# Expert stage of a two-block network: seven weight buffers, constants loaded one stage earlier, final sums of squares in column groups

## The chip, the cores and the metric

The kernel runs on one core of a Trainium2 chip, in float32. The metric is the device time of one execution in microseconds: 3112.23 us is the median of three runs before the change (3110.86 to 3115.06).

## What is computed

Two network blocks run one after the other on 512 tokens of width 1024. The change is in the last part of the second block: the merge of three branches with its residual, the router, a mixture of 16 experts and the last norm. In the reference this is

```python
merged = (sigmoid(gate_na) * (y_na @ w_branch_na) + sigmoid(gate_rw) * (y_rw @ w_branch_rw)
          + sigmoid(gate_mem) * (y_mem @ w_branch_mem))
x = x + merged @ w_out
h = rms_norm(x, norm_ffn_g)
affinity = softmax(h @ w_router)                    # 512 tokens x 16 experts
top_val, top_idx = top_k(affinity.T, 64)            # each expert takes its 64 best tokens
xe = h[top_idx]                                     # 16 x 64 x 1024
act = silu(xe @ w_gate) * (xe @ w_up)               # hidden width 2048
ye = (act @ w_down) * top_val                       # added back to the tokens taken
out = rms_norm(x + scattered(ye), norm_final_g)     # x / sqrt(mean(x*x) + 1e-6) * g
```

The weights of the 16 experts are 3 x 1024 x 2048 float32 values each, together 403 MB, all read once.

## The kernel before

The program is a row of stages, each a block with one instruction stream per engine. Between two blocks all engines meet at a barrier. Inside a block the order on an engine is the order in which the code is written, and engines wait for one another by counting semaphores. Names in the trace carry their stage: `merge_` is the function `merge_and_router`, `moe_` is `expert_ffn`; `acc` and `xg` live across both.

**The merge.** Eight branch tiles and then eight output tiles are computed on TensorE (PE), with weights (`merge_w`) loaded by SyncE (SP) into two buffers. After each output tile VectorE (DVE) adds the residual into `acc`, ScalarE (ACT) squares it (L3382) and scales it into `xg` (L3383), and TensorE multiplies `xg` with the router's weights in `route` (L3328): the eight tiles of 128 features go to four groups of 32 output partitions, which are summed later. At the end ACT copies these sums to `router_parts` (L3385) and DVE the tokens' sums of squares to `square_sums` (L3447).

**Routing.** `expert_ffn` first loads four small constants through SP (L3562: `select`, `ident`, `slots`, `gain`), then the expert weights. TensorE waits for all four (`loaded`), sums the router's four groups with `select` (L3580), and transposes tokens with `ident` (L3589). ACT makes the token scale with a logarithm and an exponential (L3728, L3730), each of which needs its own function table (ACT_TABLE_LOAD); it first waits for three memsets of DVE (`consts_ready`). DVE makes the softmax (L3800 to L3807), TensorE transposes it (L3597), and DVE copies it to `left` (L3819) and takes the 64 largest values of each expert in eight rounds of eight (L3821, L3822). The places become one-hot rows (`hot`, L3836), with which TensorE gathers the tokens (L3618) into `xe`, which lies in `xg`.

**Experts.** The hidden width is cut into 4 chunks of 512, so there are 64 chunks. A chunk `n` needs three pieces of weights, gate, up and down, of 128 x 4096 float32 = 2.097 MB each, 192 loads in all. SP issues them (L3570) into a ring of buffers:

```python
RING = 6
...
if i >= RING:                       # the piece that lay in this buffer must have been used
    if used_part == 2: sp.wait_ge(out_made, used + 1)
    else:              sp.wait_ge(hidden_made, used + 1)
```

The order of the pieces is gate 0, up 0, gate 1, up 1, down 0, gate 2, up 2, down 1, and so on. TensorE computes gate and up of a chunk side by side in two 64-partition halves of a bank (`hidden`, L3636), turns the product around (L3650), and multiplies with down (`output`, L3664). Every four chunks an expert is done; `combine` (L3689) spreads its 64 rows over the 512 tokens in four steps `q`, and DVE adds each step's two tiles into `acc` (L3861).

**The end.** After the last chunk the four steps of the last expert run. ACT squares the eight tiles of `acc` in the order in which they are done (L3778, into ring buffer 0). Then TensorE sums the squares over partitions, 8 matmuls with a 128 x 128 matrix of ones (L3716), ACT makes the scale (L3780 logarithm, L3782 exponential), DVE scales the eight tiles with `gain` (L3886), and SP stores each.

Of the kernel before, what the change touches and what calls it, by code (L numbers as in the profile page):

```python
# [7 lines left out]
P = 128  # L8
ALU = mybir.AluOpType
# [3214 lines left out]

def merge_and_router(nc, stage, y_drams, gate_dram, x_dram, w_dram, gain_dram, router_dram, acc, xg, router_parts, square_sums):

# [7 lines left out]
    with ExitStack() as ctx:  # L3234
# [15 lines left out]
        router = sb("router", [P, KT, P // ROUTER_GROUPS])  # L3250
        one = sb("one", [P, 1])
        bank = ps("bank", [P, 8, 512])

# [21 lines left out]
        sums_made = sem("sums_made")  # L3275
        parts_ready = sem("parts_ready")

        gv = gate_dram.rearrange("(b m p) t -> m p b t", b=3, p=P)
        xv = x_dram.rearrange("(m p) t -> p m t", p=P)

        with nc.Block() as block:

            @block.sync
            def _(sp):
                for g in range(tiles):
                    if g >= 2:
                        sp.wait_ge(w_ready, g - 1)
                    sp.dma_start(w[:, g % 2].rearrange("p k m -> p (k m)"), w_dram[g * P:(g + 1) * P, :]).then_inc(
                        w_loaded[g % 2], 16)
                    if g < KT:  # L3290
                        if g >= 2:
                            sp.wait_ge(gated_ready, g - 1)
                        sp.dma_start(gates[:, g % 2], gv[g]).then_inc(gates_loaded[g % 2], 16)
                    if g == 2:
                        sp.dma_start(gain[:], gain_dram).then_inc(small_loaded, 16)
                        sp.dma_start(router[:], router_dram).then_inc(small_loaded, 16)
                        sp.dma_start(acc[:], xv).then_inc(acc_loaded, 16)

            @block.tensor
# [47 lines left out]
            def _(act):  # L3347
# [27 lines left out]
                for g in range(KT, tiles):  # L3375
                    m = g - KT
                    if g + 1 < tiles:
                        split_w_high(g + 1)
                    act.wait_ge(acc_ready, m + 1)
                    if m >= 2:  # L3380
                        act.wait_ge(sq_added, m - 1)
                    nc.scalar.activation(sq[:, m % 2], acc[:, m], ACT.Square).then_inc(squared, 1)  # L3382
                    nc.scalar.activation(xg[:, m], acc[:, m], ACT.Copy, scale=gain[:, m:m + 1]).then_inc(xg_ready, 1)  # L3383
                act.wait_ge(routed, KT)
                nc.scalar.copy(router_parts[:], bank[:, 6]).then_inc(parts_ready, 1)  # L3385
# [68 lines left out]

def expert_ffn(nc, stage, acc, xg, router_parts, square_sums, select_dram, gate_dram, up_dram, down_dram, ident_dram, slots_dram,
               gain_dram, out_dram):

# [5 lines left out]
    FT = HALF // P  # L3463
    RING = 6
    BATCH = 4
    BATCHES = EXPERTS // BATCH
    CHUNKS_ALL = EXPERTS * FC
    WIDE = BATCH * CAPACITY
    with ExitStack() as ctx:
        sb, ps, sem = opener(nc, ctx, stage)  # L3470
# [6 lines left out]
        scatter = sb("scatter", [P, 2, T])  # L3477
        select = sb("select", [P, EXPERTS])
        token_scale = sb("token_scale", [P, TT])
        eps = sb("eps", [P, 1])  # L3480
        ident = sb("ident", [P, P])
        slots = sb("slots", [P, CAPACITY])
        logits = sb("logits", [P, TT, EXPERTS])
        high = sb("high", [P, TT])
        affinity = sb("affinity", [P, TT, EXPERTS])
        place_tok = sb("place_tok", [P, TT, EXPERTS])
        left = sb("left", [EXPERTS, T])
        best = sb("best", [EXPERTS, 8])
        chosen = sb("chosen", [EXPERTS, T])
        ones = sb("ones", [EXPERTS, T])  # L3490
        sg = sb("sg", [P, 2, HALF])
        act_t = sb("act_t", [P, 2, FT, CAPACITY])
        ye = sb("ye", [P, 2, HALF])
        gain = sb("gain", [P, KT])
        all_ones = sb("all_ones", [P, P])
        bank = ps("bank", [P, 8, 512])

        xe = xg[:].rearrange("p k t -> p (k t)").rearrange("p (b k n) -> p b k n", b=2, k=KT)
        sq = ring[:, 0].rearrange("p (k t) -> p k t", k=KT)
        scale = ring[:, 1, 0:T]  # L3500

        loaded = sem("loaded")
        consts_ready = sem("consts_ready")
# [26 lines left out]
        squared = sem("squared")  # L3530
        summed = sem("summed")
        final_log = sem("final_log")
        final_scale = sem("final_scale")
# [23 lines left out]
        with nc.Block() as block:  # L3557

            @block.sync
            def _(sp):  # L3560
                for dst, src in ((select[:], select_dram), (ident[:], ident_dram), (slots[:], slots_dram), (gain[:], gain_dram)):
                    sp.dma_start(dst, src).then_inc(loaded, 16)  # L3562
                for i, (n, part) in enumerate(items):
                    if i >= RING:
                        used, used_part = items[i - RING]
                        if used_part == 2:
                            sp.wait_ge(out_made, used + 1)
                        else:
                            sp.wait_ge(hidden_made, used + 1)
                    sp.dma_start(ring[:, i % RING], parts[part][n * P:(n + 1) * P, :]).then_inc(slot_loaded[i % RING], 16)  # L3570
                for j, m in enumerate(order_of):
                    sp.wait_ge(scaled, j + 1)
                    sp.dma_start(out_dram[m * P:(m + 1) * P, :], acc[:, m]).then_inc(stored, 16)
                sp.wait_ge(stored, 16 * KT)

            @block.tensor
            def _(pe):
                pe.wait_ge(loaded, 64)
                for t in range(TT):
# [116 lines left out]
                for n in range(CHUNKS_ALL + 1):  # L3696
# [13 lines left out]
                    if n >= FC + 1:  # L3710
                        combine((n - FC - 1) // FC, (n - FC - 1) % FC)
                for q in range(FT):
                    combine(EXPERTS - 1, q)
                for j, m in enumerate(order_of):
                    pe.wait_ge(squared, j + 1)
                    last = nc.tensor.matmul(bank[:, 3], all_ones[:], sq[:, m], start=(j == 0), stop=(j == KT - 1))  # L3716
                last.then_inc(summed, 1)

            @block.scalar
            def _(act):  # L3720
# [5 lines left out]

                act.wait_ge(consts_ready, 3)
                nc.scalar.activation(token_scale[:], square_sums[:], ACT.Ln, bias=eps[:, 0:1], scale=1.0 / D_MODEL).then_inc(scale_log, 1)  # L3728
# [47 lines left out]
                for j, m in enumerate(order_of):  # L3776
                    act.wait_ge(part_added, 2 * FT * (EXPERTS - 1) + j + 1)
                    nc.scalar.activation(sq[:, m], acc[:, m], ACT.Square).then_inc(squared, 1)  # L3778
                act.wait_ge(summed, 1)
                nc.scalar.activation(scale, bank[:, 3], ACT.Ln, bias=eps[:, 0:1], scale=1.0 / D_MODEL).then_inc(final_log, 1)  # L3780
                act.wait_ge(final_log, 1)
# [3 lines left out]
            def _(dve):  # L3785
                nc.vector.memset(eps[:], EPS).then_inc(consts_ready, 1)
                nc.vector.memset(all_ones[:], 1.0).then_inc(consts_ready, 1)
                nc.vector.memset(ones[:], 1.0).then_inc(consts_ready, 1)
                done = [0]
# [28 lines left out]
                dve.wait_ge(aff_turned, 1)  # L3818
                step(nc.vector.tensor_copy(left[:], bank[0:EXPERTS, 1]))  # L3819
                for r in range(CAPACITY // 8):  # L3820
                    step(nc.vector.max(best[:], left[:]))  # L3821
                    step(nc.vector.match_replace(left[:], best[:], left[:], -1.0))  # L3822
                    if r >= 1:
                        split_low(r)
                step(nc.vector.tensor_scalar(chosen[:], left[:], 0.0, None, ALU.is_lt))
                step(nc.vector.tensor_tensor_scan(left[:], ones[:], chosen[:], 0.0, ALU.mult, ALU.add))
                step(nc.vector.tensor_tensor(chosen[:], chosen[:], left[:], ALU.mult))
                assert done[0] == MOE_PLACES, done[0]
# [54 lines left out]
                dve.wait_ge(final_scale, 1)  # L3883
                dve.wait_ge(loaded, 64)
                for m in order_of:
# [21 lines left out]
def two_blocks(nc, d, out_dram):  # L3907
# [58 lines left out]
    with ExitStack() as keep:  # L3966
        acc = keep.enter_context(nc.sbuf_tensor("acc", [P, KT, SEQ], F32))
        xg = keep.enter_context(nc.sbuf_tensor("xg", [P, KT, SEQ], F32))
        router_parts = keep.enter_context(nc.sbuf_tensor("router_parts", [P, SEQ], F32))
        square_sums = keep.enter_context(nc.sbuf_tensor("square_sums", [P, SEQ // P], F32))  # L3970
        merge_and_router(nc, "merge_2", (y_na, y_mem, y_rw), g_all, x, d["w_merge_2"], d["norm_ffn_g_2"], d["router_2"], acc, xg,
                         router_parts, square_sums)
        expert_ffn(nc, "moe", acc, xg, router_parts, square_sums, d["select"], d["w_exp_gate_2"], d["w_exp_up_2"],
                   d["w_exp_down_2"], d["ident"], d["slots"], d["norm_final_g_2"], out_dram)

# [93 lines left out]
```

## Time and profile before

| | before |
|---|---|
| median of three runs | 3112.23 us (3110.86 to 3115.06) |
| the profiled execution's own time | 3112.08 us |
| its span in the profile | 3110.2 us |
| TensorE busy | 2737.7 us, 88% |
| VectorE busy | 1268.8 us, 41% |
| ScalarE busy | 801.1 us, 26% |
| DMA traffic | 628.49 MB, mean 202 GB/s |
| DMA traffic in the last third | 428 GB/s in nearly every slice |
| mean granted TensorE clock | 0.938 |

The span runs from the first to the last recorded instruction; the 1.9 us between it and the execution's time lie around it. Busy shares are means over stages with different limits: the expert stage is the last third of the span, and only there does the DMA run near 430 GB/s. Times inside the profile are microseconds from the span's start.

### The profile page before, as it was taken

What the parts mean: (1) busy time and instruction counts of PE and PEld (TensorE: products, weight loads), DVE (VectorE), ACT (ScalarE), POOL (GpSimd) and SP (SyncE); (2) the same over time, 40 slices, a digit from 0 to 9 for tenths busy, and PEclk for the clock granted to TensorE, in tenths of its full rate; (3) what the DMA queues carried; (4) which work ended last, traced back from release to release, by engine and by line L of the source; (5) the groups of instructions that cost most, each with busy time, mean ns of one, the idle gap of its engine ahead of it and who ended that gap; (6) DMA issues with size and microseconds to landing.
All of it is one profiled execution on the core that took longest, in us unless ns stands there. A gap on an engine that the chain in (4) does not pass through costs nothing. (4 is left out here: it accounts for less than half of the span.)

```text
span 3110.2 us, 45255 instructions
## 1 busy us (share of the span) xinstructions
PE 2737.7 (88%) x18876; PEld 1972.7 (63%) x18876; DVE 1268.8 (41%) x2146; ACT 801.1 (26%) x1295; POOL 110.6 (4%) x90
## 2 busy tenths in 40 slices
PE   7999877779799969899978999697899889998887
PEld 7999855479799969777867888474333333333332
DVE  5664565534256552366544333663111111111112
ACT  3212135433143331254333333342000000000001
POOL 0000011100000000000001222000000000000000
PEclk9999987789999989999989999898999999999999
DMA  4336530053433344333440000336999999999996
GB/s 136 134 134 155 119 128 21 21 198 124 147 101 115 105 151 123 105 128 130 150 152 29 1 2 1 141 116 257 428 427 428 428 427 428 428 427 428 428 428 254
DMA packets 212406, 628.49 MB, mean 202 GB/s; under 512 B 38464, under 2 KB 125632, under 8 KB 187200
## 3 DMA queue, kind: packets, MB, share of 16 engines
q1 hardware_dynamic: 179712, 573.06, 48.5%
q10 hardware_dynamic: 32512, 52.81, 4.8%
q8 instruction: 137, 2.24, 0.3%
q14 instruction: 45, 0.37, 0.0%
HBM read 577.74 MB, written 45.73 MB: 200 GB/s over the span
## 5 line engine op out<-in xcount | busy, mean ns | idle before, releaser
L3636 PE MATMUL moe_bank<-moe_ring,xg 128*64 128x512 f32 x2048 | 502.8, 636 | 93.8 <-DMA moe_ring<-in_w_exp_up 93.0
L3636 PEld LDWEIGHTS moe_bank<-moe_ring,xg 128*64 128x64 f32 x2048 | 157.4, 144 | 381.2 <-issue 372.7
L3853 DVE TENSOR_TENSOR moe_sg<-moe_sg,moe_bank 64x512 f32<-64x512 f32 x64 | 44.2, 690 | 596.6 <-ACT moe_sg L3747 596.6
L64 PE MATMUL in_bank<-in_x_low,in_w_high 128*128 128x264 f32 x896 | 259.5, 290 | 6.2 <-DVE in_w_low L1194 6.1
L66 PE MATMUL in_bank<-in_x_high,in_w_high 128*128 128x264 f32 x896 | 255.8, 286 | 0.0
L65 PE MATMUL in_bank<-in_x_high,in_w_low 128*128 128x264 f32 x896 | 255.8, 285 | 0.0
L3664 PE MATMUL moe_bank<-moe_ring,moe_act_t 128*64 128x512 f32 x1024 | 230.6, 592 | 0.5 <-ACT moe_act_t L3754 0.5
L64 PE MATMUL up_prod<-up_x_low,up_w_high 128*128 128x264 f32 x704 | 202.0, 287 | 0.0
L66 PE MATMUL up_prod<-up_x_high,up_w_high 128*128 128x264 f32 x704 | 200.9, 285 | 0.0
L65 PE MATMUL up_prod<-up_x_high,up_w_low 128*128 128x264 f32 x704 | 199.5, 283 | 0.0
L64 PEld LDWEIGHTS in_bank<-in_x_low,in_w_high 128*128 128x128 f32 x896 | 169.7, 189 | 8.2 <-DVE in_w_low L1194 7.4
L65 PEld LDWEIGHTS in_bank<-in_x_high,in_w_low 128*128 128x128 f32 x896 | 169.9, 190 | 0.3
L66 PEld LDWEIGHTS in_bank<-in_x_high,in_w_high 128*128 128x128 f32 x896 | 170.0, 190 | 0.0
L64 PE MATMUL merge_y<-merge_x_low,merge_w_high 128*128 128x264 f32 x512 | 147.6, 288 | 21.4 <-DVE merge_w_low L533 15.5
L3664 PEld LDWEIGHTS moe_bank<-moe_ring,moe_act_t 128*64 128x64 f32 x1024 | 73.4, 137 | 146.3 <-issue 145.7
L64 PE MATMUL front_bank<-front_x_low,front_w_high 128*128 128x512 f32 x368 | 148.6, 404 | 14.2 <-DVE front_w_low L2602 13.2
L3754 ACT COPY moe_act_t<-moe_bank 128x256 f32<-128x256 f32 x64 | 23.9, 373 | 527.4 <-PE moe_bank L3650 527.4
L3861 DVE TENSOR_TENSOR acc<-acc,moe_bank 128x512 f32<-128x512 f32 x128 | 82.1, 684 | 173.4 <-PE moe_bank L3689 173.4
L66 PE MATMUL merge_y<-merge_x_high,merge_w_high 128*128 128x264 f32 x512 | 146.9, 287 | 0.0
L65 PE MATMUL merge_y<-merge_x_high,merge_w_low 128*128 128x264 f32 x512 | 146.8, 287 | 0.0
L65 PE MATMUL front_bank<-front_x_high,front_w_low 128*128 128x512 f32 x368 | 144.5, 393 | 0.0
L66 PE MATMUL front_bank<-front_x_high,front_w_high 128*128 128x512 f32 x368 | 144.3, 392 | 0.0
(522 smaller groups left out, 5375.5 us busy)
## 6 DMA issues: line engine op xcount, KB each, us to landing
moe_ring<-in_w_exp_gate SPq DMA_DIRECT2D x64, 2048.0 KB, 16.7
moe_ring<-in_w_exp_up SPq DMA_DIRECT2D x64, 2048.0 KB, 21.2
moe_ring<-in_w_exp_down SPq DMA_DIRECT2D x64, 2048.0 KB, 23.0
in_w<-in_w_in SPq DMA_DIRECT2D x56, 512.0 KB, 3.5
front_w<-in_w_in SPq DMA_DIRECT2D x50, 512.0 KB, 3.4
up_w<-in_w_up SPq DMA_DIRECT2D x44, 512.0 KB, 5.1
p<-in_out ACTq DMA_DIRECT2D x48, 264.0 KB, 2.0
down_w<-in_w_down SPq DMA_DIRECT2D x8, 1408.0 KB, 8.9
```

Source lines behind the costliest of these rows:

```text
L64: nc.tensor.matmul(to, w_high, x_low, start=start, stop=False)
L65: nc.tensor.matmul(to, w_low, x_high, start=False, stop=False)
L66: return nc.tensor.matmul(to, w_high, x_high, start=False, stop=stop)
L3636: last = nc.tensor.matmul(bank[64 * g:64 * g + 64, s], xe[:, (e // BATCH) % 2, k, at:at + CAPACITY], ring[:, slot_of(n, g), k * HALF:(k + ...
L3664: last = nc.tensor.matmul(bank[64 * h:64 * h + 64, 3 + e % 2], act_t[:, s, j], ring[:, slot, at:at + HALF], start=(c == 0 and j == 0), sto ...
L3754: nc.scalar.copy(act_t[:, s].rearrange("p j n -> p (j n)"), bank[:, 2, s * FT * CAPACITY:(s + 1) * FT * CAPACITY]).then_inc(act_t_ready, 1)
L3853: nc.vector.tensor_tensor(sg[0:CAPACITY, s], sg[0:CAPACITY, s], bank[64:64 + CAPACITY, s], ALU.mult).then_inc(act_ready, 1)
L3861: nc.vector.tensor_tensor(acc[:, FT * h + q], acc[:, FT * h + q], bank[:, part_bank(e, q) + h], ALU.add).then_inc(part_added, 1)
```

## The change

Four edits, all in the merge and the expert stage:

1. `RING` is 7 instead of 6. To make room, `left`, `chosen` and `ones` are laid into `sg` and `ye`, which are not in use yet during routing.
2. The four constants are loaded during the merge, by SP after the weights of its ninth tile; the expert stage no longer waits for them.
3. ACT runs a logarithm of a single column at the end of the merge (`warm`), so that its function table is in place when the expert stage starts. DVE makes one more constant (`group_rows`, 1/32 everywhere) ahead of `ones`, and ACT waits for four memsets instead of three.
4. The final sums of squares are 8 matmuls of 32 output partitions (L3718 in the new file), the j-th into column group j mod 4, the first two ahead of the last combine. The four groups are copied to SBUF by ACT and summed and spread over all partitions by one more matmul with `group_rows` (L3729).

```diff
@@ merge_and_router, SP @@
                         sp.dma_start(acc[:], xv).then_inc(acc_loaded, 16)
+                    if g == KT:
+                        for dst, src in constants:
+                            sp.dma_start(dst, src).then_inc(constants_loaded, 16)
+                sp.wait_ge(constants_loaded, 16 * len(constants))
@@ merge_and_router, ACT @@
+                act.wait_ge(one_ready, 1)
+                nc.scalar.activation(warm[:], one[:], ACT.Ln).then_inc(parts_ready, 1)
                 act.wait_ge(routed, KT)
                 nc.scalar.copy(router_parts[:], bank[:, 6]).then_inc(parts_ready, 1)
@@ expert_ffn @@
-    RING = 6
+    RING = 7
+    GROUP = P // 4
...
+        sums = ring[:, 2, 0:T]
+        left, chosen, ones = sg[0:EXPERTS, 0], sg[0:EXPERTS, 1], ye[0:EXPERTS, 0]
@@ SP @@
-                for dst, src in ((select[:], select_dram), (ident[:], ident_dram), (slots[:], slots_dram), (gain[:], gain_dram)):
-                    sp.dma_start(dst, src).then_inc(loaded, 16)
@@ TensorE @@
-                pe.wait_ge(loaded, 64)
...
+                def sum_squares(j):
+                    pe.wait_ge(squared, j + 1)
+                    at = GROUP * (j % 4)
+                    nc.tensor.matmul(bank[at:at + GROUP, 3], all_ones[:, 0:GROUP], sq[:, order_of[j]], start=(j < 4),
+                                     stop=(j >= 4)).then_inc(summed, 1)
+
                 for q in range(FT):
                     combine(EXPERTS - 1, q)
-                for j, m in enumerate(order_of):
-                    pe.wait_ge(squared, j + 1)
-                    last = nc.tensor.matmul(bank[:, 3], all_ones[:], sq[:, m], start=(j == 0), stop=(j == KT - 1))
-                last.then_inc(summed, 1)
+                    if q >= 2:
+                        for j in range(2 * q - 4, 2 * q - 2):
+                            sum_squares(j)
+                for j in range(KT - 4, KT):
+                    sum_squares(j)
+                pe.wait_ge(sums_ready, 1)
+                nc.tensor.matmul(bank[:, 4], group_rows[:], sums, start=True, stop=True).then_inc(spread, 1)
@@ ACT @@
-                act.wait_ge(consts_ready, 3)
+                act.wait_ge(consts_ready, 4)
...
-                act.wait_ge(summed, 1)
-                nc.scalar.activation(scale, bank[:, 3], ACT.Ln, bias=eps[:, 0:1], scale=1.0 / D_MODEL).then_inc(final_log, 1)
+                act.wait_ge(summed, KT)
+                nc.scalar.copy(sums, bank[:, 3]).then_inc(sums_ready, 1)
+                act.wait_ge(spread, 1)
+                nc.scalar.activation(scale, bank[:, 4], ACT.Ln, bias=eps[:, 0:1], scale=1.0 / D_MODEL).then_inc(final_log, 1)
@@ DVE @@
+                nc.vector.memset(group_rows[:], 1.0 / GROUP).then_inc(consts_ready, 1)
-                nc.vector.memset(ones[:], 1.0).then_inc(consts_ready, 1)
+                nc.vector.memset(ones, 1.0).then_inc(consts_ready, 1)
```

On SyncE's queue, from the last merge weights to the first expert weights, before the change:

```order
L3293 DMA merge_gates<-p 128x3x512
L3288 DMA merge_w<-in_w_merge 128x1024 x8
L3281 UNCONDITIONAL_BRANCH
L3559 UNCONDITIONAL_BRANCH
L3562 DMA moe_select<-in_select 128x16
L3562 DMA moe_ident<-in_ident 128x128
L3562 DMA moe_slots<-in_slots 128x64
L3562 DMA moe_gain<-in_norm_final_g 128x8
L3570 DMA moe_ring<-in_w_exp_gate 128x4096
```

and with it:

```order
L3296 DMA merge_gates<-p 128x3x512
L3291 DMA merge_w<-in_w_merge 128x1024
L3303 DMA select<-in_select 128x16
L3303 DMA ident<-in_ident 128x128
L3303 DMA slots<-in_slots 128x64
L3303 DMA final_gain<-in_norm_final_g 128x8
L3291 DMA merge_w<-in_w_merge 128x1024 x7
L3284 UNCONDITIONAL_BRANCH
L3565 UNCONDITIONAL_BRANCH
L3574 DMA moe_ring<-in_w_exp_gate 128x4096
L3574 DMA moe_ring<-in_w_exp_up 128x4096
```

The four constants now stand between the ninth and the tenth load of merge weights, and the expert weights are the first DMAs after the barrier (the two branches are the ends of the blocks).

On ScalarE, from the end of the merge to the token scale, before:

```order
L3383 ACTIVATE xg<-acc,merge_gain 128x512
L3385 COPY router_parts<-merge_bank 128x512
L3281 UNCONDITIONAL_BRANCH
L3719 UNCONDITIONAL_BRANCH
L3728 ACT_TABLE_LOAD
L3728 ACTIVATE moe_token_scale<-square_sums,moe_eps 128x4
L3730 ACT_TABLE_LOAD
```

and with the change:

```order
L3390 ACTIVATE xg<-acc,merge_gain 128x512
L3392 ACT_TABLE_LOAD
L3392 ACTIVATE merge_warm<-merge_one 128x1
L3394 COPY router_parts<-merge_bank 128x512
L3284 UNCONDITIONAL_BRANCH
L3731 UNCONDITIONAL_BRANCH
L3740 ACTIVATE moe_token_scale<-square_sums,moe_eps 128x4
L3742 ACT_TABLE_LOAD
L3742 ACTIVATE moe_token_scale<-moe_token_scale 128x4
```

One of the two table loads, the one for the logarithm, has moved ahead of the copy of `router_parts`, together with a small logarithm of `merge_one`.

On TensorE, the last instructions of the program, before:

```order
L3689 MATMUL moe_bank<-moe_scatter,moe_ye 128x512 x2
L3650 MATMUL moe_bank<-moe_ident,moe_sg 128x64 x4
L3664 MATMUL moe_bank<-moe_ring,moe_act_t 64x512 x8
L3689 MATMUL moe_bank<-moe_scatter,moe_ye 128x512 x10
L3716 MATMUL moe_bank<-moe_ring,moe_all_ones 128x512 x8
```

and with the change:

```order
L3653 MATMUL moe_bank<-ident,moe_sg 128x64 x4
L3667 MATMUL moe_bank<-moe_ring,moe_act_t 64x512 x8
L3692 MATMUL moe_bank<-moe_scatter,moe_ye 128x512 x8
L3718 MATMUL moe_bank<-moe_ring,moe_all_ones 32x512 x2
L3692 MATMUL moe_bank<-moe_scatter,moe_ye 128x512 x2
L3718 MATMUL moe_bank<-moe_ring,moe_all_ones 32x512 x6
L3729 MATMUL moe_bank<-moe_ring,moe_group_rows 128x512
```

Two of the eight sums (now 32 output partitions instead of 128) stand ahead of the last expert's last combine, six behind it, and one matmul over all partitions follows.

## Rows read from the trace of the kernel before

**Rows 1.** Weight stream by stretch: us; busy PE, PEld, DVE, ACT, POOL; clock, DMA share, GB/s.

```profile
2113.00:2142.00 29.00, 11.50 (x53) 9.68 (x53) 23.15 (x45) 5.61 (x9) 0.00 (x0) 0.56 1.00 425
2142.50:2158.50 16.00, 15.28 (x90) 10.99 (x91) 0.00 (x0) 3.63 (x5) 0.00 (x0) 0.89 0.00 0
2163.00:3063.00 900.00, 807.23 (x3670) 287.76 (x3668) 137.00 (x207) 74.73 (x150) 0.00 (x0) 0.96 1.01 428
```

**Rows 2.** SyncE's queue in order of time: start us, us, instruction.

```profile
2109.20 0.33 SPq L3562 DMA_DIRECT2D moe_select<-in_select  x1
...
2113.88 0.46 SPq L3570 DMA_DIRECT2D moe_ring<-in_w_exp_gate  x1
2158.70 0.33 SPq L3570 DMA_DIRECT2D moe_ring<-in_w_exp_up  x1
```

**Rows 3.** Chain of waits, first and last expert chunks: start us, us, what.

```profile
2151.58 10.52 PE moe_bank L3636 x48
...
3046.98 21.19 DMA moe_ring<-in_w_exp_up
...
3068.30 3.65 PE moe_bank L3636 x16
```

**Rows 4.** All engines in order of time, from merge to routing.

```profile
2105.94 0.71 ACT L3383 ACTIVATE xg<-acc,merge_gain 128x512 f32<-128x512 f32 x1
2107.79 0.59 ACT L3385 COPY router_parts<-merge_bank 128x512 f32<-128x512 f32 x1 [1.14 <-PE merge_bank L3328]
2108.77 0.16 DVE L3447 COPY square_sums<-merge_bank 128x4 f32<-128x4 f32 x1 [2.01 <-PE merge_bank L3343]
...
2109.55 0.48 DVE L3788 MEMSET moe_ones<- 16x512 f32 x1
2110.51 0.30 ACT L3728 ACTIVATE moe_token_scale<-square_sums,moe_eps 128x4 f32<-128x4 f32 x1
2110.83 1.28 ACT L3730 ACT_TABLE_LOAD   x1
2112.12 0.21 ACT L3730 ACTIVATE moe_token_scale<-moe_token_scale 128x4 f32<-128x4 f32 x1
...
2112.24 1.89 PE L3580 MATMUL moe_bank<-moe_select,router_parts 128*128 128x16 f32 x8 [3.51 <-DMA moe_gain<-in_norm_final_g]
2114.17 0.23 DVE L3800 TENSOR_TENSOR moe_logits<-moe_bank,moe_token_scale 128x64 f32<-128x64 f32 x1 [4.13 <-PE moe_bank L3580]
...
2115.16 0.69 ACT L3724 ACTIVATE moe_z_tok<-moe_bank,moe_token_scale 128x512 fp32r<-128x512 f32 x1 [2.84 <-PE moe_bank L3589]
2115.75 0.25 ACT L3734 ACTIVATE moe_logits<-moe_logits 128x64 f32<-128x64 f32 x1
...
2116.57 0.23 DVE L3807 TENSOR_TENSOR moe_affinity<-moe_logits,moe_high 128x64 f32<-128x64 f32 x1
...
2117.42 1.06 PE L3597 MATMUL moe_bank<-moe_ident,moe_affinity 128*16 128x128 f32 x4
...
2118.51 0.68 DVE L3819 COPY moe_left<-moe_bank 16x512 f32<-16x512 f32 x1 [0.93 <-PE moe_bank L3597]
```

**Rows 5.** TensorE in the merge, around one router matmul.

```profile
2091.28 1.05 PE L3328 MATMUL merge_bank<-xg,merge_router 128*32 128x512 f32 x2
2092.26 0.50 PE L64 MATMUL merge_bank<-merge_m_low,merge_w_high 128*128 128x512 f32 x1
```

**Rows 6.** VectorE, ScalarE and TensorE, the final sums.

```profile
3088.48 5.00 DVE L3861 TENSOR_TENSOR acc<-acc,moe_bank 128x512 f32<-128x512 f32 x8 [1.31 <-PE moe_bank L3689]
3089.26 4.88 ACT L3778 ACTIVATE moe_ring<-acc 128x512 f32<-128x512 f32 x8 [8.19 <-DVE acc L3861]
3099.25 0.69 ACT L3780 ACTIVATE moe_ring<-moe_bank,moe_eps 128x512 f32<-128x512 f32 x1 [3.80 <-PE moe_bank L3716]
3089.82 2.33 PE L3689 MATMUL moe_bank<-moe_scatter,moe_ye 64*128 64x512 f32 x8 [0.52 <-DVE acc L3861]
3092.07 7.13 PE L3716 MATMUL moe_bank<-moe_ring,moe_all_ones 128*128 128x512 f32 x16
```

More of the change, by code:

```diff
@@ L3222, with merge_and_router @@
 ROUTER_GROUPS = 4
-def merge_and_router(nc, stage, y_drams, gate_dram, x_dram, w_dram, gain_dram, router_dram, acc, xg, router_parts, square_sums):
+def merge_and_router(nc, stage, y_drams, gate_dram, x_dram, w_dram, gain_dram, router_dram, constants, acc, xg, router_parts,
+                     square_sums):
     T = SEQ
@@ L3251, in merge_and_router @@
         one = sb("one", [P, 1])
+        warm = sb("warm", [P, 1])
         bank = ps("bank", [P, 8, 512])
@@ L3276, in merge_and_router @@
         parts_ready = sem("parts_ready")
+        constants_loaded = sem("constants_loaded")
         gv = gate_dram.rearrange("(b m p) t -> m p b t", b=3, p=P)
@@ L3452, with expert_ffn @@
 EXPERT_FF = 2 * D_MODEL
-def expert_ffn(nc, stage, acc, xg, router_parts, square_sums, select_dram, gate_dram, up_dram, down_dram, ident_dram, slots_dram,
-               gain_dram, out_dram):
+def expert_ffn(nc, stage, acc, xg, router_parts, square_sums, select, ident, slots, gain, gate_dram, up_dram, down_dram, out_dram):
     T = SEQ
@@ L3477, in expert_ffn @@
         scatter = sb("scatter", [P, 2, T])
-        select = sb("select", [P, EXPERTS])
         token_scale = sb("token_scale", [P, TT])
         eps = sb("eps", [P, 1])
-        ident = sb("ident", [P, P])
-        slots = sb("slots", [P, CAPACITY])
         logits = sb("logits", [P, TT, EXPERTS])
@@ L3486, in expert_ffn @@
         place_tok = sb("place_tok", [P, TT, EXPERTS])
-        left = sb("left", [EXPERTS, T])
         best = sb("best", [EXPERTS, 8])
-        chosen = sb("chosen", [EXPERTS, T])
-        ones = sb("ones", [EXPERTS, T])
         sg = sb("sg", [P, 2, HALF])
@@ L3493, in expert_ffn @@
         ye = sb("ye", [P, 2, HALF])
-        gain = sb("gain", [P, KT])
         all_ones = sb("all_ones", [P, P])
+        group_rows = sb("group_rows", [P, P])
         bank = ps("bank", [P, 8, 512])
@@ L3500, in expert_ffn @@
         scale = ring[:, 1, 0:T]
-        loaded = sem("loaded")
+        sums = ring[:, 2, 0:T]
+        left, chosen, ones = sg[0:EXPERTS, 0], sg[0:EXPERTS, 1], ye[0:EXPERTS, 0]
         consts_ready = sem("consts_ready")
@@ L3531, in expert_ffn @@
         summed = sem("summed")
+        sums_ready = sem("sums_ready")
+        spread = sem("spread")
         final_log = sem("final_log")
@@ L3818, in _ @@
                 dve.wait_ge(aff_turned, 1)
-                step(nc.vector.tensor_copy(left[:], bank[0:EXPERTS, 1]))
+                step(nc.vector.tensor_copy(left, bank[0:EXPERTS, 1]))
                 for r in range(CAPACITY // 8):
-                    step(nc.vector.max(best[:], left[:]))
-                    step(nc.vector.match_replace(left[:], best[:], left[:], -1.0))
+                    step(nc.vector.max(best[:], left))
+                    step(nc.vector.match_replace(left, best[:], left, -1.0))
                     if r >= 1:
                         split_low(r)
-                step(nc.vector.tensor_scalar(chosen[:], left[:], 0.0, None, ALU.is_lt))
-                step(nc.vector.tensor_tensor_scan(left[:], ones[:], chosen[:], 0.0, ALU.mult, ALU.add))
-                step(nc.vector.tensor_tensor(chosen[:], chosen[:], left[:], ALU.mult))
+                step(nc.vector.tensor_scalar(chosen, left, 0.0, None, ALU.is_lt))
+                step(nc.vector.tensor_tensor_scan(left, ones, chosen, 0.0, ALU.mult, ALU.add))
+                step(nc.vector.tensor_tensor(chosen, chosen, left, ALU.mult))
                 assert done[0] == MOE_PLACES, done[0]
@@ L3883, in _ @@
                 dve.wait_ge(final_scale, 1)
-                dve.wait_ge(loaded, 64)
                 for m in order_of:
@@ L3970, in two_blocks @@
         square_sums = keep.enter_context(nc.sbuf_tensor("square_sums", [P, SEQ // P], F32))
[L3971 to L3974, printed above, removed]
+        select = keep.enter_context(nc.sbuf_tensor("select", [P, EXPERTS], F32))
+        ident = keep.enter_context(nc.sbuf_tensor("ident", [P, P], F32))
+        slots = keep.enter_context(nc.sbuf_tensor("slots", [P, CAPACITY], F32))
+        gain = keep.enter_context(nc.sbuf_tensor("final_gain", [P, KT], F32))
+        constants = ((select[:], d["select"]), (ident[:], d["ident"]), (slots[:], d["slots"]), (gain[:], d["norm_final_g_2"]))
+        merge_and_router(nc, "merge_2", (y_na, y_mem, y_rw), g_all, x, d["w_merge_2"], d["norm_ffn_g_2"], d["router_2"], constants,
+                         acc, xg, router_parts, square_sums)
+        expert_ffn(nc, "moe", acc, xg, router_parts, square_sums, select, ident, slots, gain, d["w_exp_gate_2"], d["w_exp_up_2"],
+                   d["w_exp_down_2"], out_dram)
 def by_partition(a):
```

## The prediction

> **What bounds the kernel now.** I read the busy shares by stretch first, then SyncE's queue at the two ends of the expert stage, then the chain of waits, and last all engines in order of time where the change touches them. The stretches show a stage with one limit: for 900 us the DMA engines are busy the whole time (share 1.01) at 428 GB/s, while TensorE has 807 us of work [rows 1]. A load of weights is 2.097 MB, so it takes 2.097 / 0.428 = 4.90 us, and 192 of them 941 us. The reader is to see where this stream does not run: from 2142.5 to 2158.5 it moves nothing [rows 1]. SyncE's queue says why: the sixth load is issued at 2113.88, and the seventh only at 2158.70, because it waits until the first chunk's matmuls have used their buffer [rows 2]. Those start at 2151.58 [rows 3], at the end of routing. So the stage is: routing, then the first `hidden`, then the stream restarts and runs without a break until the last chunk, whose matmuls start at 3068.30, when the load issued at 3046.98 has landed after 21.19 us [rows 3]. What follows is the tail. Three things can therefore move the end: how many loads are done before the restart, when the restart comes, and how long the tail is.
>
> **Edit 1, the seventh buffer.** The seventh load no longer waits. It is issued right behind the sixth and runs in the empty stretch, where there are 16 us for its 4.90 us [rows 1]. The restart then has 185 loads before it instead of 186. The stream has a backlog at every moment until the end (share 1.01), so the whole 4.90 us come off the landing of the last weights. Releases stay in time: the first chunk frees two buffers at once, 9.8 us of stream, and the next chunk's matmuls take less than that. In the steady stage a deeper ring buys nothing, since the DMA is full anyhow. **Minus 4.9 us.** Bounds: 0, if the last landing were not set by the restart, to 4.9; a loss is rival E.
>
> **Edits 2 and 3, an earlier start of routing.** Before, TensorE's first matmul starts at 2112.24 after 3.51 us in which it waited for the last constant [rows 4], while SyncE's first instruction after the barrier stands at 2109.20 [rows 2]. Without that wait it starts at about 2109.3, 2.9 us earlier. Its chain to the copy of `left` at 2118.51 [rows 4] is: router sums 1.89, then 3.3 of transposes, then the turn of `affinity` 1.06, together 6.24 us from 2112.24, which would end at 2115.5. The other chain into that turn goes through the token scale. Of the logarithm's two table loads one goes, but ACT now waits for four memsets, of which `ones` is the last: it started at 2109.55 and took 0.48 [rows 4]. A 128-column memset ahead of it adds about 0.2, so `ones` ends at 2110.25, and the logarithm starts there instead of at 2110.51. So the warm table saves 0.25 us, not 1.28. Logarithm 0.30, table load 1.28 and exponential 0.21 follow, and the scale stands at 2112.1 instead of 2112.33. The first softmax step then starts at 2112.2 instead of 2114.17. Before, the softmax's exponential waited for ACT's first token copy (2115.16 plus 0.69, exponential at 2115.75); now that copy starts with the scale at 2112.15, since the transposes are done by then, and the exponential runs at 2113.0. From exponential to the end of `affinity` it was 2115.75 to 2116.80, 1.05 us [rows 4], so `affinity` is there at 2114.0 and TensorE's transposes, ending at 2114.5, are the later of the two. The turn and the copy follow: `left` at about 2115.3, **3.2 us earlier**. From there to the first chunk's matmuls it is 2151.58 - 2118.51 = 33.1 us [rows 3, 4], mostly one long row of DVE steps in which nothing changes, and the restart comes as much earlier. Bounds: 2.5, if the barrier opens 0.4 later and the transposes run as slowly as before, to 3.9, if the granted clock, 0.56 in that stretch [rows 1], stays at its higher level because TensorE no longer idles. A part that starts at another clock phase in the gather is within that.
>
> What this moves elsewhere: the four constants stand on SyncE's queue in the merge, between the loads of the ninth and the tenth tile. Four issues like that of 2109.20, about 0.4 us each, delay the tenth load by under 2 us; the expert stage's own loads come 1.8 us earlier, which the empty stretch hides. I cost both at nothing; if the tenth tile had no slack, it would be 2 us. On ACT the warm-up stands in front of the copy of `router_parts`. The last scaling ends at 2105.94 + 0.71 = 2106.65; table load 1.28 and a small logarithm of 0.2 to 0.3 end at 2108.2; the copy, 0.59, ends at 2108.8 instead of 2108.38. DVE's last instruction ends at 2108.93 [rows 4], so the barrier stays where it was. **Nothing**, with 0.15 us to spare.
>
> The rows have no idle time around a table load: the logarithm ends at 2110.81, the load starts at 2110.83 and the exponential follows at 2112.12 [rows 4]. The Trainium skill (ScalarE: Activation LUTs, section "What ACT_TABLE_LOAD costs") adds a drain of about 1.38 us to each load of 1.28 us. By that rule the merge's barrier would come some 1.3 us later, and the sum would be 3104.1 as an estimate; the trace does not agree, and I give it little.
>
> **Edit 4, the sums.** Before: eight sums of 7.13 us start at 3092.07 behind the last combine, and the logarithm starts at 3099.25 [rows 6]. DVE's eight adds run without a gap from 3088.48, 0.625 each, and ACT's squares follow them, 0.61 each, to 3094.14 [rows 6]. After: the third combine ends at 3090.9 and the first two squares are ready at 3090.5. The two sums go into different column groups; the pairs of `hidden` and `combine` matmuls run side by side in this kernel: 8 records of combine, two combines, in 2.33 us [rows 6], where each record alone takes about 0.45 (7.13 / 16). So I take 1.0 us for two or four sums, until 3091.95. The last combine moves from 3091.01 to 3092.0 and ends at 3093.1, the last add at 3094.4, the last square at 3095.05, all 0.9 later than before. The middle four sums end by 3094.3, the last one at 3096.05. Then come the copy, 0.6 as that of `router_parts`, to 3096.7, and the spreading matmul, 0.9 plus 0.2 of hand-over, to 3097.85. The logarithm's table load, which before lay beside the sums, now follows the copy: 3096.7 + 1.28 = 3098.0. The logarithm starts there instead of at 3099.25: **minus 1.2 us**. Bounds: minus 2.1, if the first two sums don't hold the last combine up (last sum at 3095.15, then the same 1.95 us); plus 1.8, if the sums run one after another at 0.89 each (rival B).
>
> A change of tile shape costs little in the rows: a router matmul of 32 columns starts at 2091.28, and the next 128-column one 0.98 later [rows 5], against 0.89 for a float32 matmul in a row of its like [rows 6]. The Trainium skill (TensorEngine Tiling (Array Packing), section "Key Properties") says that a change of the tiling mode drains the engine, which speaks against sums put between combines. By the row that is 0.1 us for each of three changes; were it a whole matmul each time, the gain of 1.2 would be gone.
>
> **The sum.** 4.9 + 3.2 + 1.2 = 9.3 us, against the profiled execution's 3112.08, which is 0.15 below the median of the runs shown: 3102.8 us.
>
> **Rivals.**
> B. The column groups run one after another. Sums of 0.89 each: the last combine would end at 3093.9, the middle four at 3097.4, the last two at 3099.2, and with copy and spreading the logarithm would start at 3101.05, 1.8 late. Time 3105.8. For it: no row has four groups of 32 at once. Against: the combine rows.
> C. The last landing does not follow the restart, so the seventh buffer gives nothing: 3107.7. For it: a load takes 21.19 us to land, more than four at full rate, so its slowest part may run on another schedule. Against: no stall in 900 us.
> D. The barrier comes 1.3 us later through the warm-up: 3104.1.
> E. **Slower.** With one more load in flight the stream runs at a lower rate, through 185 loads or 906 us. It eats the gain of 9.3 from 1.03% on, 428 down to 423.6 GB/s; at 2% the time is 3102.8 + 18.1 = 3120.9. For it: nothing measured with seven. Against: 425 GB/s in the first fill, when the number in flight falls from six to none, and 428 later [rows 1].
> F. The change does not do what it says for routing, because the token scale decides and not the constants: 0.2 instead of 3.2, 3105.8.
>
> **How the numbers follow.** Forecast 0.76 (its own range 3100 to 3105.5), B 0.09, C 0.05, D 0.03, E 0.04, F 0.03. A measurement of this kernel tells about 0.2% from no change, 6.2 us, so faster is below 3106.0. That holds for the forecast, D and half of B and F: 0.85. C, the other halves and a small E are no change: 0.12. A large E is slower: 0.03. Runs of one kernel lie up to 3 us above their median, so the range goes from 3099.5 (upper bounds of all terms 3101.2, less 1.5 of run-to-run difference) to 3107.5, short of C.
>
> **What would show it.** Right: seven weight loads issued in a row right after the barrier, an empty stretch of about 10 us instead of 16 (16 - 4.9 + 1.8 - 3.2), the eighth load at about 2155.5, `left` at 2115.3, the last chunk's matmuls at about 3060.2, the logarithm 29.8 us behind them instead of 30.95. Wrong: a rate under 428 GB/s in the stage, sums of 0.9 us each, a barrier after 2109.2, or a last chunk less than 7 us earlier.

## The result and the profile after

The changed kernel takes 3095.57 us (median of six runs, 3093.32 to 3097.03) against 3113.64 us before (six runs, 3107.98 to 3118.66): a ratio of 0.9942, 95% interval 0.9930 to 0.9955. The forecast was 3102.8 with a range from 3099.5 to 3107.5: right in its sign, but the gain is 18 us and not 9.

Five marks in the two profiles cut the span into stretches:

| stretch | before | after | difference | forecast |
|---|---|---|---|---|
| start of the span to SyncE's first expert instruction | 2109.20 | 2108.71 | -0.5 | 0 |
| from there to the copy of `left` | 9.31 | 6.03 | -3.3 | -3.2 |
| to the first chunk's matmuls | 33.07 | 31.97 | -1.1 | 0 |
| to the first release of a buffer | 7.12 | 7.12 | 0 | 0 |
| to the landing of the last chunk's up weights | 909.47 | 898.38 | -11.1 | -4.9 |
| to the end of the span | 42.03 | 40.79 | -1.2 | -1.2 |
| span | 3110.2 | 3093.0 | -17.2 | -9.3 |

The weight stream by stretch, columns as in [rows 1]:

```profile
2144.00:2154.00 10.00, 9.28 (x51) 4.78 (x51) 0.00 (x0) 2.62 (x4) 0.00 (x0) 1.00 0.05 23
2163.00:3040.00 877.00, 786.57 (x3619) 281.65 (x3617) 136.28 (x206) 73.55 (x147) 0.00 (x0) 0.97 1.01 431
```

The long stretch runs at 431 GB/s where it ran at 428 [rows 1]. The window before the restart still holds the last packets of the first fill (23 GB/s); the stream itself stands still for some 9 us, where about 10 were forecast. The first fill does not differ: the 425 in [rows 1] is the mean of a window that takes in both ends of the fill. Inside it the rates are 433 before and 431 after:

```profile
2118.00:2136.00 18.00, 4.43 (x19) 2.94 (x16) 16.89 (x33) 3.10 (x5) 0.00 (x0) 0.59 1.01 433
2118.00:2136.00 18.00, 3.95 (x16) 2.64 (x16) 16.68 (x31) 2.06 (x3) 0.00 (x0) 0.54 1.01 431
```

SyncE's queue and the chain of waits, to be held against [rows 2, 3]:

```profile
2108.71 0.33 SPq L3574 DMA_DIRECT2D moe_ring<-in_w_exp_gate  x1
...
2111.98 0.47 SPq L3574 DMA_DIRECT2D moe_ring<-in_w_exp_up  x1
2153.83 0.33 SPq L3574 DMA_DIRECT2D moe_ring<-in_w_exp_down  x1
```

```profile
2146.71 10.52 PE moe_bank L3639 x48
...
3032.57 19.64 DMA moe_ring<-in_w_exp_up
...
3052.35 3.65 PE moe_bank L3639 x16
```

Seven loads go out in a row, the eighth 41.9 us later. 185 loads take 898.38 us, 4.856 each; before it was 186 loads in 909.47, 4.890 each. One load less is 4.9 us of the difference, the 0.033 us on each of 185 loads the other 6.2.

All engines between merge and routing, against [rows 4]:

```profile
2106.18 1.28 ACT L3392 ACT_TABLE_LOAD   x1
...
2107.58 0.57 ACT L3394 COPY router_parts<-merge_bank 128x512 f32<-128x512 f32 x1
2108.28 0.16 DVE L3456 COPY square_sums<-merge_bank 128x4 f32<-128x4 f32 x1 [2.01 <-PE merge_bank L3350]
...
2108.76 1.59 PE L3583 MATMUL moe_bank<-select,router_parts 128*128 128x16 f32 x8 [0.52 <-PEq L3284]
...
2109.20 0.48 DVE L3803 MEMSET moe_ye<- 16x512 f32 x1
2109.72 0.30 ACT L3740 ACTIVATE moe_token_scale<-square_sums,moe_eps 128x4 f32<-128x4 f32 x1 [1.57 <-DVE moe_ye L3803]
...
2110.03 1.28 ACT L3742 ACT_TABLE_LOAD   x1
...
2111.33 0.20 ACT L3742 ACTIVATE moe_token_scale<-moe_token_scale 128x4 f32<-128x4 f32 x1
...
2111.64 0.23 DVE L3815 TENSOR_TENSOR moe_logits<-moe_bank,moe_token_scale 128x64 f32<-128x64 f32 x1 [1.95 <-ACT moe_token_scale L3742]
...
2113.24 0.23 DVE L3822 TENSOR_TENSOR moe_affinity<-moe_logits,moe_high 128x64 f32<-128x64 f32 x1
2113.64 1.06 PE L3600 MATMUL moe_bank<-ident,moe_affinity 128*16 128x128 f32 x4
2114.74 0.68 DVE L3834 COPY moe_sg<-moe_bank 16x512 f32<-16x512 f32 x1 [0.49 <-PE moe_bank L3600]
```

The warm logarithm's table load and the copy of `router_parts` end before DVE's last instruction of the merge, so the barrier opens 0.27 us behind that as before. TensorE starts 0.05 behind the barrier instead of 3.04. The logarithm (L3740) waits for the last memset, not for a table. The turn of `affinity` (L3600) follows TensorE's own transposes and not DVE, which has `affinity` ready 0.17 earlier.

TensorE and ScalarE at the end, against [rows 6]:

```profile
3073.86 1.13 PE L3692 MATMUL moe_bank<-moe_scatter,moe_ye 64*128 64x512 f32 x4 [0.52 <-DVE acc L3876]
3074.92 1.05 PE L3718 MATMUL moe_bank<-moe_ring,moe_all_ones 128*32 128x512 f32 x4
3075.90 1.13 PE L3692 MATMUL moe_bank<-moe_scatter,moe_ye 64*128 64x512 f32 x4
3076.96 1.12 PE L3718 MATMUL moe_bank<-moe_ring,moe_all_ones 128*32 128x512 f32 x8
3078.48 1.64 PE L3718 MATMUL moe_bank<-moe_ring,moe_all_ones 128*32 128x512 f32 x4 [0.40 <-ACT moe_ring L3790]
3080.80 1.12 PE L3729 MATMUL moe_bank<-moe_ring,moe_group_rows 128*128 128x512 f32 x2 [0.68 <-ACT moe_ring L3792]
```

```profile
3080.16 0.58 ACT L3792 COPY moe_ring<-moe_bank 128x512 f32<-128x512 f32 x1 [1.14 <-PE moe_bank L3718]
3080.77 1.28 ACT L3794 ACT_TABLE_LOAD   x1
3082.06 0.69 ACT L3794 ACTIVATE moe_ring<-moe_bank,moe_eps 128x512 f32<-128x512 f32 x1
```

Two sums, four records, take 1.05 us and four sums 1.12, where one sum alone took 0.89 before (7.13 / 8): column groups run side by side. From the last chunk's first matmul (3052.35) to the logarithm it is 29.71 us; before 30.95.

### The profile page after: what moved, and what is told of

Same layout as the page of the kernel before. It is cut to its first block and busy times, and to the rows that moved or that the text cites. A ratio compares the mean times of both kernels' runs of the same rounds, so it can differ in the third digit from the quotient of the medians.

```text
span 3093.0 us, 45262 instructions
## 1 busy us (share of the span) xinstructions
PE 2727.7 (88%) x18878; PEld 1971.1 (64%) x18878; DVE 1268.4 (41%) x2147; ACT 799.9 (26%) x1297; POOL 110.6 (4%) x90
## 5 line engine op out<-in xcount | busy, mean ns | idle before, releaser
L3639 PE MATMUL moe_bank<-moe_ring,xg 128*64 128x512 f32 x2048 | 492.3, 624 | 93.0 <-DMA moe_ring<-in_w_exp_up 92.1
```

The costliest lines, as they stand in the source:

```text
L3639: last = nc.tensor.matmul(bank[64 * g:64 * g + 64, s], xe[:, (e // BATCH) % 2, k, at:at + CAPACITY], ring[:, slot_of(n, g), k * HALF:(k + ...
```

## The experiments

The 6.2 us had no term in the forecast. Loading the constants earlier also keeps them in SBUF ahead of the ring, 864 bytes per partition. The built programs put the ring's first byte at 51360 before, 160 past a multiple of 256, and at 52224 after, a multiple of 512. So there were three theories: the place of the ring, the seventh load in flight, or a difference between runs. The barrier into the expert stage lies between 2105.5 and 2116.0 in the profiles of the ten kernels tried, though no edit lies ahead of the merge, so stretches inside a profile decide, not total times. (The medians of the first four kernels came out within 3 us of what was expected of them, some above and some below.)

**The place of the ring alone.**

```diff
+        pad = sb("pad", [P, 88])        # 352 bytes; the kernel before
         ring = sb("ring", [P, RING, FT * D_MODEL])
```

> The kernel before, with 352 unused bytes ahead of the ring, so that its rows begin at byte 51712 of each partition (a multiple of 512) instead of 51360 (32 past a multiple of 64). Six buffers, all else as before. The stretch from the seventh load's issue to the last chunk's first matmul was 909.6 us before (186 loads of 4.890) and is 898.5 after the change (185 loads of 4.857). If the rate hangs on where the ring begins: 186 x 4.857 = 903.4, 431 GB/s, and 6 us less in all, about 3107 against 3113.6. If it hangs on the number of loads in flight, or differs from run to run: 909.6, 428 GB/s, no change in time.

It took 3105.06 us, ratio 0.9977 (0.9967 to 0.9988). The stage between 2200 and 3000, columns as in [rows 1]:

```profile
2200.00:3000.00 800.00, 716.71 (x3288) 256.47 (x3286) 125.78 (x190) 67.08 (x134) 0.00 (x0) 0.97 1.01 431
```

186 loads in 903.25 us, 4.856 each: the place alone gives the whole difference in rate. (The `pad` moves the ring and, with it, every tile declared behind it; the two were not moved apart.)

**The old place in the changed kernel.**

```diff
+        pad = sb("pad", [P, 40])        # 160 bytes; the changed kernel
```

> The changed kernel, with 160 unused bytes ahead of the ring: it begins at byte 52384, 160 past a multiple of 512 as in the kernel before; seven buffers. If the rate hangs on where the ring begins: the stretch from the first release to the last chunk is 185 x 4.890 = 904.6 instead of 898.5, 428 GB/s, time about 3101.7 against 3095.6. If on the loads in flight: 898.5, 431 GB/s, 3095.6.

3098.95 us, 0.9955 (0.9942 to 0.9968); 185 loads in 904.89, 4.891 each, with seven in flight:

```profile
2200.00:3000.00 800.00, 718.12 (x3268) 257.74 (x3270) 125.69 (x190) 66.60 (x133) 0.00 (x0) 0.96 1.01 428
```

**Six buffers at the new place.**

```diff
-    RING = 7
+    RING = 6
```

> The changed kernel with RING = 6 and the ring at the same byte, 52224. If the seventh buffer is worth one load and the rate hangs on the place: 186 x 4.857 = 903.4, 431 GB/s, time 4.9 more than the changed kernel, about 3100.4. If the seventh buffer also made the rate: 909.6, 428 GB/s, 11 more, about 3106.6.

3103.09 us, 0.9962 (0.9950 to 0.9975); 186 loads in 903.20, 4.856 each. The seventh buffer is worth one load, 903.20 - 898.38 = 4.8 us, and does nothing to the rate:

```profile
2200.00:3000.00 800.00, 717.47 (x3284) 256.73 (x3286) 125.11 (x189) 66.55 (x134) 0.00 (x0) 0.96 1.01 431
```

**Which places are fast.** The changed kernel with 64, 256 and 128 bytes ahead of the ring (`pad` of 16, 64 and 32 values).

> The changed kernel with 64 unused bytes ahead of the ring: byte 52288, a multiple of 64 but not of 128. If a multiple of 64 is enough for the rate: 898.5 us for the stretch and 3095.6 in all. If a multiple of 512 is needed: 904.6 and about 3101.7. If the place does not matter: 898.5.

> The changed kernel, ring at byte 52480, a multiple of 256 but not of 512. A ring at 64 past a multiple of 512 was slow (904.75 us for 185 loads), at 0 fast (898.4). If 256 is enough: 898.4 us, 431 GB/s. If 512 is needed: 904.8, 428 GB/s.

> The changed kernel, ring at byte 52352, 128 past a multiple of 512. Fast so far: 0 and 256 past it, 898.1 to 898.4 us for 185 loads. Slow: 64 and 160, 904.8. If 128 is enough: 898.3. If 256 is needed: 904.8.

The stage between 2200 and 3000 with 64, 256 and 128 bytes:

```profile
2200.00:3000.00 800.00, 715.73 (x3258) 256.64 (x3256) 126.38 (x191) 66.69 (x133) 0.00 (x0) 0.96 1.01 428
```

```profile
2200.00:3000.00 800.00, 717.47 (x3288) 257.77 (x3286) 127.07 (x192) 67.28 (x134) 0.00 (x0) 0.97 1.01 430
```

```profile
2200.00:3000.00 800.00, 716.66 (x3264) 257.32 (x3262) 125.69 (x190) 66.71 (x133) 0.00 (x0) 0.96 1.01 428
```

| first byte of the ring, mod 512 | kernel | loads | release to last landing, us | us per load |
|---|---|---|---|---|
| 160 | before | 186 | 909.47 | 4.890 |
| 0 | changed | 185 | 898.38 | 4.856 |
| 0 | before, padded | 186 | 903.25 | 4.856 |
| 0 | changed, six buffers | 186 | 903.20 | 4.856 |
| 256 | changed, padded | 185 | 898.08 | 4.855 |
| 64 | changed, padded | 185 | 904.75 | 4.891 |
| 128 | changed, padded | 185 | 904.41 | 4.889 |
| 160 | changed, padded | 185 | 904.89 | 4.891 |

The two multiples of 256 are fast, the other three places cost 0.7%, all three the same. A difference between runs is out: the four kernels below all have the ring at 0 and take 898.1 to 898.4 us for their 185 loads, and the three slow kernels with 185 loads lie within 0.5 us of one another. The runs come from three chips, and two of these show both a fast and a slow place. (The padded kernel with 64 took 3103.73 us, 0.9973, 0.9961 to 0.9985; the other two have one run each, 3100.95 and 3097.44.)

The place does not cost from the first byte on. The traces record each 16 KB row of a weight load as one packet. From 2118 to 2130, early in the first fill, every such packet took 611 ns, in the kernel before as in the changed one. From 2200 to 3000 the mean is 615.4 before, with 12% of the packets at 611, and 611.7 in the changed kernel, with nearly all at 611. At all four slow rings the packets begin to grow longer some 25 us after the stream starts, and again some 25 us after it restarts. What sets in then is not shown by any run.

**Constants late again** (edit 2 undone).

```diff
+                for dst, src in constants:              # expert_ffn, SP, ahead of the weights
+                    sp.dma_start(dst, src).then_inc(loaded, 16)
...
+                pe.wait_ge(loaded, 64)                  # TensorE, ahead of the router's sums
```

> The changed kernel with edit 2 undone: the four constants are loaded at the start of the expert stage again, ahead of the weights, and TensorE waits for them; the warm logarithm stays. The copy of left started 9.3 us after the expert stage's first SyncE instruction before the change and 6.0 after it. If the wait for the constants was worth the 3.3: 9.3. If the warm table was worth 1.3 of it: 8.0.

3100.58 us in one run. From SyncE, TensorE and DVE in order of time:

```profile
2111.34 0.33 SPq L3564 DMA_DIRECT2D select<-in_select  x1
...
2114.45 1.89 PE L3582 MATMUL moe_bank<-select,router_parts 128*128 128x16 f32 x8 [3.57 <-DMA final_gain<-in_norm_final_g]
...
2119.27 0.60 PE L3599 MATMUL moe_bank<-ident,moe_affinity 128*16 128x128 f32 x4
...
2119.91 0.68 DVE L3833 COPY moe_sg<-moe_bank 16x512 f32<-16x512 f32 x1
```

`left` comes 8.57 after the barrier, between the two numbers. TensorE starts 3.11 after it as before the change (3.04), so the wait is back, and it is worth 3.0 of the 3.3 us. That `left` does not come at 9.3 is the clock: from TensorE's start to `left` it is 5.46 instead of 6.27, because the granted clock rose 7.5 us behind the barrier instead of 9.5, and the turn of `affinity` took 0.60 instead of 1.06 [rows 4]. In the changed kernel the clock stood at half (0.50) from 2109.7 until behind the start of `left`, and the turn took 1.06 as before. The other 0.3 of the 3.3 us are the router's sums, 1.59 there against 1.89 [rows 4]; in the first microsecond behind the barrier the clock was still 0.68.

**No warm table** (edit 3 undone: the two lines of `warm` removed).

> The changed kernel without the warm logarithm (edit 3), so that the expert stage's first logarithm loads its table again. From the expert stage's first SyncE instruction to the copy of left: 6.0 us with the warm-up. If the memsets and TensorE's transposes stand in the way anyway, the scale comes 0.3 later and left at 6.0 to 6.3. If the table load was on the path: 7.3.

3094.68 us in one run.

```profile
2108.84 0.33 SPq L3572 DMA_DIRECT2D moe_ring<-in_w_exp_gate  x1
2108.85 1.28 ACT L3738 ACT_TABLE_LOAD   x1 [0.84 <-PEq L3284]
...
2110.15 0.30 ACT L3738 ACTIVATE moe_token_scale<-square_sums,moe_eps 128x4 f32<-128x4 f32 x1
...
2111.76 0.20 ACT L3740 ACTIVATE moe_token_scale<-moe_token_scale 128x4 f32<-128x4 f32 x1
...
2113.95 0.61 PE L3598 MATMUL moe_bank<-ident,moe_affinity 128*16 128x128 f32 x4 [0.57 <-DVE moe_affinity L3820]
2114.59 0.67 DVE L3832 COPY moe_sg<-moe_bank 16x512 f32<-16x512 f32 x1
```

The scale is ready 3.1 after the barrier instead of 2.8, and `left` comes after 5.75, against 6.03 with the warm-up. The two can't be compared as they stand, since the clock rose earlier here (from 2112.80 on it is 1.00). But the table load of 1.28 us is not on the path: it runs beside the memsets and costs the scale 0.3. In the changed kernel the warm-up is worth at most 0.2 by estimate: without it `affinity` would be ready at 2113.8 instead of 2113.47, and the turn started at 2113.64 behind TensorE's transposes. Here, with those done earlier, TensorE waited for `affinity`, so the warm-up would have saved up to 0.3.

**The old sums** (edit 4 undone).

```diff
-    ...
+                for j, m in enumerate(order_of):
+                    pe.wait_ge(squared, j + 1)
+                    last = nc.tensor.matmul(bank[:, 3], all_ones[:], sq[:, m], start=(j == 0), stop=(j == KT - 1))
```

> The changed kernel with edit 4 undone: eight sums of 128 output partitions behind the last combine, as before; all else as changed. From the last chunk's first matmul to the final logarithm it was 30.95 us before the change and 29.71 with it. If the new sums gave the difference: 30.95. If the tail was shorter for another reason, such as the granted clock: 29.7.

3096.79 us in one run. The chain of waits:

```profile
3053.02 3.65 PE moe_bank L3639 x16
...
3076.86 7.08 PE moe_bank L3719 x16
...
3083.96 0.69 ACT moe_ring L3783
```

3083.96 - 3053.02 = 30.94 us: the sums give 1.23.

**A busier TensorE ahead of the gather.** Left over was the 1.1 us between `left` and the first chunk. All of it lies in the gather, 64 records, 10.31 us before and 9.22 after. Its first 5 us before and after, columns as in [rows 1] (the clock third from the end):

```profile
2140.60:2145.60 5.00, 5.00 (x24) 5.00 (x25) 0.52 (x1) 0.59 (x1) 0.00 (x0) 0.50 0.28 115
```

```profile
2136.80:2141.80 5.00, 5.00 (x31) 5.00 (x32) 0.55 (x1) 0.59 (x1) 0.00 (x0) 0.70 1.02 433
```

Half clock all through in the one, part of the time full in the other. No edit changes an instruction of the gather. In the padded and undone kernels it took 9.20 to 10.33. The next kernel tries to hold the clock up:

```diff
+                for _ in range(6):                      # ahead of the places' transposes
+                    nc.tensor.matmul(bank[:, 7], ident[:], xg[:, 0], start=True, stop=True)
```

> The changed kernel with six float32 matmuls whose results nobody uses, on TensorE in the idle stretch before the gather. The gather's 64 records took 9.2 to 10.3 us in the kernels so far, and the granted clock in it rose from half to full after 3 to 5 us. If the idle stretch is what keeps the clock at half: the gather in about 8 us, the first chunk 1.2 to 2.3 earlier behind the copy of left (31 instead of 32 to 33 us), and the whole 1 to 2 us less. If not: 32 to 33 us, no change.

3096.59 us, 0.9953 (0.9937 to 0.9969), no better than the change; gather 9.15 us, first chunk 31.71 behind `left`. The extra matmuls, the pause behind them, and the gather's first 5 us:

```profile
2129.20:2136.90 7.70, 7.64 (x13) 2.96 (x12) 7.45 (x15) 0.69 (x1) 0.00 (x0) 0.70 0.99 423
2136.90:2139.10 2.20, 0.00 (x0) 0.00 (x0) 2.13 (x3) 0.00 (x0) 0.00 (x0) 1.00 1.04 447
2141.30:2146.30 5.00, 4.98 (x31) 5.00 (x32) 0.60 (x1) 0.59 (x1) 0.00 (x0) 0.72 1.03 436
```

The clock rose during the matmuls and stood at full in the pause, but the gather still had part of its start at half. It did not do what it was meant for.

## Why the prediction was wrong

- **Edit 1** said that the stream after the restart is "185 loads" of 4.90 us and that "In the steady stage a deeper ring buys nothing". Both hold for the ring's depth: 4.8 us by the six-buffer kernel. The step that failed is the unsaid one beside it: that a load takes the same time before and after. Edit 2 moved the ring by 864 bytes per partition, from 160 past a multiple of 256 to a multiple of it, and each of 185 loads became 0.033 us faster, 6.2 us in all. Rival E had the right quantity and the wrong sign: it priced a rate 1% lower at 9.3 us, and the range allowed nothing for a higher one. The 425 GB/s that it read in the first fill is a mean over both ends of the fill, not its rate; inside the fill it is 433. Without these 6.2 us the change would have come to 11.0, inside the range.
- I followed what each edit does to instructions and queues and not to addresses. No row of the trace shows an address; the order of the allocations in the code does, since the constants now stand ahead of the ring. What a place costs could not be read from the trace of before, which has one place. One sign was there: the same stream took 611 ns a packet in the first fill and 615.4 in the long stretch.
- The Trainium skill has a rule on places (DMA: Bandwidth & Descriptors, section "How a descriptor splits into AXI transactions"): a descriptor that does not start at a multiple of 256 bytes pays for a first transaction that begins at the boundary below. The runs agree on the 256 in the long stretch. They differ from the Trainium skill's count of beats, which grows with the offset, since 64, 128 and 160 cost the same, and no packet is longer early in the first fill, so that rule is not shown to be the cause. Between a kernel and its padded twin only places in SBUF differ, so the loss hangs on the SBUF side; how it comes about stays open.
- **Edits 2 and 3**: 3.3 us against 3.2, with the path as forecast: TensorE 0.05 behind the barrier, logarithm behind the memsets, barrier unmoved, TensorE's transposes later than `affinity`. The closeness is in part luck. The working's own chain, 6.24 us from a start 2.9 earlier, ends 2.9 earlier and not 3.2; the rest came from router sums at a clock that had not yet fallen. Of the 3.3, 3.0 are the wait for the constants. The bound of 3.9 rested on a clock that stays up when TensorE does not idle; it fell to 0.50 within a microsecond of the barrier, with TensorE 94% busy in that microsecond. No drain stands around the warm table load (2106.18 + 1.28, the logarithm at 2107.47), so rival D is out.
- **Edit 4**: 1.24 us against 1.2, confirmed by undoing it; rival B is out.
- 1.1 us in the gather and 0.5 ahead of the stage came on top. The first is the clock's phase, which the forecast had held to 0.7; why it differs from kernel to kernel stays open. The second is within what the stage's start varies by.
- The range's lower end, 3099.5, is 0.2 below the sum given for it (3101.2 - 1.5 = 3099.7); nothing hangs on that.

## What to carry to other kernels

Where a stage is bound by a DMA stream, look at where its target tiles begin: here 0 and 256 bytes past a multiple of 512 gave some 431 GB/s and 64, 128 and 160 gave 428, and small tiles declared ahead of the ring decided it. Any edit that adds, removes or resizes a tile can move those behind it, so an experiment on such a stage should print or pin the address. Count a prefetch buffer by the empty stretch that it fills, one load's time (4.8 us here), and expect nothing from it where the DMA is busy already. Before a window's mean is taken for a rate, narrow it until it holds no start or end of the stream.

## What the hardware showed that I had not expected

The rate of a saturated stream of 16 KB rows hung on its place in SBUF, 4.856 us per 2.097 MB at the two multiples of 256 bytes and 4.890 at the three other places, with a DMA share of 1.01 in both cases, so the busy share does not show the loss. And it did so only from some 25 us into the stream on; from 2118 to 2130 every packet took 611 ns at either kind of place. And six matmuls that brought the granted clock to full did not keep it there through a pause of some 2 us and the start of the gather (0.72 over 5 us, against 0.70 without them).
